# An earlier square root in two split norms, and relu evictions ahead of the squaring in two MLP heads

## What is computed

```python
def rms_norm(x, g):
    y = xf * lax.rsqrt(jnp.mean(xf * xf, axis=-1, keepdims=True) + NORM_EPS)
    return (y * g.astype(jnp.float32)).astype(x.dtype)

def sq_relu_mlp(h, w1, w2):
    return jnp.square(jax.nn.relu(h @ w1)) @ w2

        xl = xl + mod_l[2][:, None, :] * ol
        hl = modulate(rms_norm(xl, norm2_g[i]), mod_l[3], mod_l[4])
        xl = xl + mod_l[5][:, None, :] * sq_relu_mlp(hl, w_ff1[i], w_ff2[i])
```

## Time and profile before

| | |
|---|---|
| median of 3 runs | 2323.17 us (2319.16 to 2323.88) |
| the profiled execution's own time | 2324.08 us |
| its span | 2322.3 us |
| mean granted TensorE clock | 0.972 of full speed |
| TensorE matmul busy | 2212.4 us (95% of the span) |
| VectorE busy | 1370.6 us (59%) |
| ScalarE busy | 794.8 us (34%) |
| GpSimd busy | 719.5 us (31%) |
| chain that ended last | PE 84%, DVE 8%, DMA 3%, ACT 2%, POOL 1%, issue 1% |

### The profile page before, as it was taken

One profiled execution on the slowest core, in us unless ns is written; L12 is line 12 of the kernel. 1 busy time (PEld: TensorE's weight loads), 2 busy tenths in 40 slices (PEclk: granted clock), 3 DMA queues, 4 the chain that ended last, 5 costly groups with the idle time before them and its releaser, 6 DMA issues.

```text
span 2322.3 us, 31326 instructions
## 1 busy us (share of the span) xinstructions
PE 2212.4 (95%) x11982; PEld 1864.6 (80%) x11982; DVE 1370.6 (59%) x1796; ACT 794.8 (34%) x1100; POOL 719.5 (31%) x417
## 2 busy tenths in 40 slices
PE   6999899899999999998999999999997999799997
PEld 5887588899999999784447888887886888688885
DVE  5789842745444444544663745645327551799997
ACT  3211143111111112325663211212323533677775
POOL 1133304233333334322335344444442234111111
PEclk8999979999999999999999999999998999899999
DMA  9699931622222222120002333333231134599996
GB/s 312 198 274 275 284 104 55 262 64 64 63 63 63 63 64 73 57 64 1 10 1 64 101 97 93 99 91 113 74 94 56 60 86 154 204 394 406 399 406 251
DMA packets 254616, 328.53 MB, mean 141 GB/s; under 512 B 15022, under 2 KB 200879, under 8 KB 242231
## 3 DMA queue, kind: packets, MB, share of 16 engines
q1 hardware_dynamic: 242524, 291.65, 38.2%
q0 software_dynamic: 6688, 25.69, 2.9%
q10 hardware_dynamic: 5307, 9.83, 1.1%
HBM read 299.16 MB, written 27.98 MB: 141 GB/s over the span
## 4 chain that ended last, share of the span: by engine, by line
PE 84%; DVE 8%; DMA 3%; ACT 2%; POOL 1%; issue 1%; ACTq 0%; SPq 0%; POOLq 0%; DVEq 0%
PE acc L632 47%; PE acc L3059 8%; PE pb L3077 4%; PE acc L2566 3%; PE pa L2795 2%; PE acc L2781 2%; DMA mod_raw<-in_w_mod 2%; PE pb L2808 2%; PE acc L686 2%; PE acc L668 2%; PE pb L2517 1%; PE acc L2630 1%; DVE hid_hi L1857 1%; PE pa L2456 1%; PE acc L715 1%
## 5 line engine op out<-in xcount | busy, mean ns | idle before, releaser
L571 POOL TENSOR_TENSOR wlo<-raw,whi 128x1024 fp32r<-128x1024 f32 x192 | 480.0, 2502 | 1031.7 <-ACT whi L560 1011.9
L560 ACT ACTIVATE whi<-raw 128x1024 fp32r<-128x1024 f32 x188 | 199.1, 1060 | 892.6 <-PE acc L632 830.5
L632 PE MATMUL acc<-ah,whi 128*128 128x384 f32 (+1 forms) x1256 | 393.3, 361 | 2.6 <-DVE sg L2054 2.6
L632 PE MATMUL acc<-al,whi 128*128 128x384 f32 (+1 forms) x1256 | 388.5, 357 | 0.0
L632 PE MATMUL acc<-ah,wlo 128*128 128x384 f32 (+1 forms) x1256 | 388.4, 357 | 0.0
L632 PEld LDWEIGHTS acc<-ah,whi 128*128 128x128 f32 x1256 | 230.4, 189 | 30.4 <-issue 10.6
L632 PEld LDWEIGHTS acc<-ah,wlo 128*128 128x128 f32 x1256 | 231.3, 188 | 20.1
L632 PEld LDWEIGHTS acc<-al,whi 128*128 128x128 f32 x1256 | 231.1, 188 | 20.1 <-issue 0.5
L1877 DVE SCALAR_TENSOR_TENSOR x<-acc,mod,x 128x512 f32<-128x512 f32 (+1 forms) x174 | 109.7, 658 | 232.2 <-PE acc L632 232.1
L1060 DVE TENSOR_TENSOR expert_lo<-expert_pair,expert_hi 128x1024 fp32r<-128x1024 f32 x192 | 224.4, 1219 | 14.5 <-ACT expert_hi L1055 14.5
L1055 ACT ACTIVATE expert_hi<-expert_pair 128x1024 fp32r<-128x1024 f32 x192 | 201.4, 1059 | 63.5 <-PE acc L3059 40.0
(11 more groups left out here) (495 smaller groups left out, 3672.4 us busy)
## 6 DMA issues: line engine op xcount, KB each, us to landing
raw<-in_w_ff SPq DMA_DIRECT2D x128, 512.0 KB, 3.9
mod_raw<-in_w_mod SPq DMA_DIRECT2D x80, 512.0 KB, 7.9
expert_pair<-in_expert_w_gate SPq DMA_DIRECT2D x32, 1024.0 KB, 7.8
expert_pair<-in_expert_w_up SPq DMA_DIRECT2D x32, 1024.0 KB, 7.5
expert_pair<-in_expert_w_down SPq DMA_DIRECT2D x32, 1024.0 KB, 7.2
raw<-in_w_in SPq DMA_DIRECT2D x30, 512.0 KB, 3.8
raw<-in_conv_w_pw SPq DMA_DIRECT2D x24, 512.0 KB, 12.2
expert_rows_dram<-zero_rows POOLq DMA_DIRECT2D x1, 12288.0 KB, 38.1
```

Of the source, the lines that this page charges most:

```text
L560: e.eng.activation(whi[e.n["q"] % 2][:, :], raw[r][:, :], ACT.Copy).then_inc(S["hi_ready"], 1)
L571: e.eng.tensor_tensor(wlo[b][:, :], raw[e.n["g"] % RING][:, :], whi[b][:, :].bitcast(F32), ALU.subtract).then_inc(S["lo_ready"], 1)
L632: ins = e.eng.matmul(o, w, m, start=keys.index(key) == n, stop=len(keys) - 1 - keys[::-1].index(key) == n)
```

## The change

The change has three parts.

The first: in `split_norm_act` ScalarE takes the early square root behind two late squares (`ahead`) and no longer behind all of the first `FIRST_SPLIT` of them. In norms 1 and 3 three late squares move behind the root. In norms 2 and 4, where `FIRST_SPLIT` is 2, nothing moves.

The second: in both MLP heads VectorE takes the three early results and the late results of slots 0 and 1 out of PSUM first, with the maximum alone (`positive`), into three separate buffers (`rstd`, `tmp` and `tmp3`). Then it squares and splits slots 0 and 1 (`square`), takes slot 2's late result, and squares and splits slot 2. Number and kind of the instructions are the same.

The third: `zero_rows` is set behind the first MLP's head and not in front of it, and GpSimd issues its transfer four low parts (weight slots) later.

```diff
--- before.py
+++ after.py
@@ -823,11 +823,14 @@
                 e.eng.wait_ge(S["sq_added_early"], (KT - 2) * early + i - 2)
             e.eng.activation((squares[(i - 1) % 2] if i else square_sum[0])[:, c0:c1], x[:, i, c0:c1], ACT.Square
                              ).then_inc(S["sq_early"], 1)
-        for i in range(FIRST_SPLIT[n]):
+        ahead = min(2, FIRST_SPLIT[n])
+        for i in range(ahead):
             square_late(i)
         e.eng.wait_ge(S["root_in_early"], early + 1)
         e.eng.activation(token_stat[:, c0 // P:c1 // P], token_stat[:, c0 // P:c1 // P], ACT.Sqrt
                          ).then_inc(S["root_out_early"], 1)
+        for i in range(ahead, FIRST_SPLIT[n]):
+            square_late(i)
         squares_late(-1)
         for i in range(KT):
             e.eng.wait_ge(S["x_scaled_early"], KT * early + i + 1)
@@ -1632,10 +1635,11 @@
 
         slots(e, KT - 1 - SPLIT_SLOTS, low, units=0)
         split_norm_pool(e, 1)
+        split_only(e, 4, low)
         pool.wait_ge(S["prepared"], 4)
         pool.dma_start(yo_d.rearrange("(j p) d -> p j d", p=P),
                        zero_rows[:, :].unsqueeze(1).to_broadcast([P, LIST, D])).then_inc(S["rows_zeroed"], 16)
-        split_only(e, 64 - 2 * SPLIT_SLOTS, low)
+        split_only(e, 60 - 2 * SPLIT_SLOTS, low)
         split_norm_pool(e, 2)
         slots(e, 12 - SPLIT_SLOTS, low, units=0)
 
@@ -1861,13 +1865,33 @@
                 square_of_relu(token_cols(take_unit(e), c0) if c0 else all_cols(take_unit(e)), b, j, c0, TOK).then_inc(S["hid_ready"], 1)
 
             def head():
+
+                def positive(values, j, s0, s1):
+                    free_unit(e, TS(parts[j][:, s0:s1], values, 0.0, None, ALU.max))
+
+                def square(j, s0, s1):
+                    e.step(TT(tmp2[:, s0:s1], parts[j][:, s0:s1], parts[j][:, s0:s1], ALU.mult))
+                    e.step(dve.tensor_copy(hid_hi[0][:, j, s0:s1], tmp2[:, s0:s1]))
+                    return TT(hid_lo[0][:, j, s0:s1], tmp2[:, s0:s1], hid_hi[0][:, j, s0:s1].bitcast(F32), ALU.subtract)
+
+                parts = (rstd, tmp, tmp3)
                 for j in range(SPLIT_SLOTS):
                     values = early_cols(n, take_unit(e)) if j < 2 else after_unit(e, third_cols())
-                    square_of_relu(values, 0, j, EARLY[n][0], EARLY[n][1])
-                for j in range(SPLIT_SLOTS):
-                    square_of_relu(late_cols(n, take_unit(e)), 0, j, LATE[n][0], LATE[n][1]).then_inc(S["hid_ready"], 1)
-                    e.n["g"] += 1
-                    e.n["q"] += 1
+                    positive(values, j, EARLY[n][0], EARLY[n][1])
+                for j in range(2):
+                    positive(late_cols(n, take_unit(e)), j, LATE[n][0], LATE[n][1])
+                dve.wait_ge(S["acc_free"], e.at("u", 2))
+                for j in range(2):
+                    square(j, EARLY[n][0], EARLY[n][1])
+                    square(j, LATE[n][0], LATE[n][1]).then_inc(S["hid_ready"], 1)
+                positive(late_cols(n, take_unit(e)), 2, LATE[n][0], LATE[n][1])
+                dve.wait_ge(S["acc_free"], e.at("u", 2))
+                square(2, EARLY[n][0], EARLY[n][1])
+                square(2, LATE[n][0], LATE[n][1]).then_inc(S["hid_ready"], 1)
+                e.n["g"] += SPLIT_SLOTS
+                e.n["q"] += SPLIT_SLOTS
+                if n == 1:
+                    dve.memset(zero_rows[:, :], 0.0).then_inc(S["prepared"], 1)
 
             def down(chunk, j, b):
                 for n in (2 * j, 2 * j + 1):
@@ -1892,7 +1916,6 @@
         e.step(scales(3, 1, 4, V_N2B))
 
         operand_done(e, 3)
-        dve.memset(zero_rows[:, :], 0.0).then_inc(S["prepared"], 1)
         def last_rows_of_first():
             dve.wait_ge(S["rows_zeroed"], 16)
             split_norm(2, 5, 4, 3, to_stream_part(40), AFFINE[2])
```

## The result

The changed kernel takes 2308.4 us (median of 4 runs, 2302.94 to 2309.11), beside 2321.76 us for the kernel before (4 runs, 2319.16 to 2323.88). The ratio is 0.9938, with a 95% interval of 0.9919 to 0.9957: faster by 0.6%. The median lies 3.4 us over the predicted 2305.0 and inside the range. The profiled execution took 2302.94 us, with a span of 2301.2, and the others up to 2309.11. TensorE is busy for 2202.5 us (96%), where it was 2212.4, carries 87% of the chain that ended last, and its mean granted clock is 0.977. The two profiled executions are 21.1 us apart, the medians 13.4: the profile of after is the fastest of its runs, and that of before is slower than each of the runs beside it.

A forecast was written before the change was run, and what follows sets the result against it. TensorE, busy for 95% of the span, was taken as the bound, so only its waits and the lower clock behind them give time back. 9.6 + 3.7 + 5.6 - 0.8 = 18.1 us from 2323.17 gave 2305, range 2301 to 2309.

The forecast's parts named there:

- First head: First MLP head: TensorE's 7.44 us eviction wait falls to 0.4 and 2.6 of lower clock goes; 9.6 us gained.
- Second head: Second MLP head: the 2.39 us eviction wait and 1.6 of lower clock go, less 0.3 remaining; 3.7 us gained.
- Norm 1's root: Norm 1: root ready before TensorE asks, so the 2.64 us wait and 3.0 of lower clock go; 5.6 us gained.
- Norm 3's root: Norm 3: a new wait before the late squares' sums, with the lower clock behind it; 0.8 us lost.
- The zeros' transfer: GpSimd's 38.1 us transfer moves from the head into the steady part, with weight loads still in time; nothing gained.
- The sum: Whole kernel: 9.6 + 3.7 + 5.6 - 0.8 = 18.1 us gained, from the median 2323.17 to 2305.
- the first: Rival on norm 3: the last addition is not late, 6.1 us instead of -0.8, so 2298; chance 0.12.
- The second: Rival: norm 1 ends as norm 3 does, or 0.4 us waits lower the clock in the heads; 2310; chance 0.15.
- The third: Rival on the heads: the wait only changes its name, TensorE lacking something else at 422; 2311 to 2314; chance 0.05.
- the fourth: Rival on the steady part: slower, the zeros starve the weight ring; chance 0.03.
- the fifth: Rival on the whole kernel: no change that can be measured; chance 0.04.

The follow-up runs named there:

- zeros not moved: The change's roots and evictions against the kernel before, with the zeros set and written at their old place: 2305.43 us, 0.9937.
- Issue alone: The kernel before with only GpSimd's issue of the zeros four low parts later, the memset staying: 2315.66 us, 0.9967.
- earlier additions: The changed kernel with norm 3's last two additions to `x` further ahead: 2302.25 us, 0.9922 against the kernel before.
- roots alone: The kernel before with only the first part of the change, the earlier square roots: 2316.54 us, 0.9978.
- heads alone: The kernel before with only the second part, evictions first in both MLP heads; memset and transfer of zeros left in place: 2308.49 us, 0.995.
- zeros alone: The kernel before with only the third part, memset and transfer of zeros behind the first head: 2316.74 us, 0.9983.

## Why the prediction was right, step by step

**First head, 9.6 us:** 7.34 + 2.30 = 9.64 in every profile that has the evictions first. The mechanism was right; that the sum is exact is luck, since two terms miss by the same 0.3: the remaining wait is 0.10 us and not 0.4, and the lower clock had cost 2.3 and not 2.6. The explanation was incomplete in one step: the cast of 6.08 us was taken as one that GpSimd's low parts hold, but no other instruction of the head stood through two of them, and this one had come while GpSimd was issuing the transfer. The forecast did not rest on that: in "zeros not moved" evictions take 0.41 us during the issue and 0.69 beside a low part, as they do elsewhere.

**Second head, 3.7 us:** 3.75 measured, with a wait of 0.16 us: 2.23 of the wait and 1.5 of the clock. The latter is a draw as well. "Issue alone" has the same wait and pays nothing for it, so that against the mean of the three profiles with a wait of 2.4 us (0, 0.0 and 1.5) the part is worth 3.3.

**Norm 1's root, 5.6 us:** 5.72 in every profile with the root moved. But 3.0 of it was the price of the lower clock in one execution, and other executions of the same code paid less, see below. Set against the mean of the four profiles with the root behind five squares (0, 2.8, 1.5 and 1.5 us ahead of the trace before), it is worth 4.3.

**Norm 3's root, -0.8 us:** the mechanism was right and the sizes were off, so that against the trace before the three profiles of the change gain 0.1 to 0.55 us and lose nothing. The new wait stands where it was forecast, before the sums, with the lower clock behind. TensorE is idle for 3.5 us, 3.12 and the 0.41 for `head_lo`, and not for 4.7. Two terms of the sum differ. TensorE took up the sums at 1261.52, which with the 14.33 us gained until then is 1275.85 in the trace before: 2.15 us before 1278.00, not 1.4. Two `al` tiles slipped in ahead of `head_lo` and not one, though `head_lo`, which was taken as staying in its place, ended 0.6 us later (1256.65 + 14.33 = 1270.98, not 1270.34). And the fall of the clock then cost 1.6 us (2.15 - 0.55) to 2.1 (2.15 - 0.08), not 2.2. Over all profiles of this place the early root gains -0.6 to 1.2 us (mean 0.3 of five) and the late one 0 to 1.3 (mean 0.7 of five), so the root alone is worth some -0.4, which the scatter does not tell from 0.

The rule of the Trainium skill (SBUF — State Buffer, Who interferes with whom), by which the two engines exclude each other for a whole instruction, agrees with the `al` tile at 1254.71, which ends 0.28 us behind GpSimd's low part.

**The zeros' transfer, nothing:** right beside the other two parts, as far as these runs can tell (2305.43 without the move, 2303.5 and 2303.6 with it, intervals overlapping). The transfer took 39.1 us where the earlier trace rows have 38.1, and ScalarE waited for no weights beside it. It was issued at 442.47 us, 23.8 us later than before, where some 30 were forecast. The row of the changed kernel's issues:

```profile
expert_rows_dram<-zero_rows POOLq DMA_DIRECT2D x1, 12288.0 KB, 39.1
```

Alone the move is worth 4.0 us of the first head, since the cast's long stand goes with the issue's place.

**The sum, 18.1 us:** the four terms come to 19.2 to 19.7 us in the profiles. The column "between" takes 1.7 back, in eleven of the twelve other profiles and whatever the edit: the trace before had less of the lower clock between the first head and norm 3 than all of them but one. For the same matmuls it needs 822.0 us there and the change 823.8; "earlier additions", which has the whole change in it, needs 822.0 again. So the 1.7 us are luck of that execution and not a cost of the change. "Start" and "rest", which the change doesn't touch either, add 3.1 to 5.4 us in the three profiles. The medians differ by 13.4, 18.1 and 17.6 us.

That the forecast of 18.1 meets the second of these to the tenth is luck in part. With each price taken from all profiles that have the old wait, and not from the one before, the terms are 4.3 and -0.4 as above, 3.3 for the second head and 9.4 for the first (there "roots alone" has the same wait and pays 0.4 less): an estimate of 16.6 us, inside the spread of the three medians, whose mean is 16.3.

Of the rivals, the first (norm 3 gives 6.1 us) is refuted by the new wait; by the traces 4.3 us are to be had with the additions moved, and 5.3 to 5.5 with the sums moved as well. The second is right in one respect: a short wait can be followed by a lower clock. It did not happen in these heads. The third and the fourth did not occur, and the fifth (no change) is outside the interval.

## What to carry to other kernels

An engine that reads results out of PSUM for TensorE should take all of them that are ready before it works on any, when buffers allow: it costs no instruction and gave 13 of the 18 us. Before a wait is removed, look for what the next instruction behind it will ask for, and move that too: norm 3's root was worth nothing that the scatter lets one see until two additions had moved, and then 4 to 5 us by the traces (1.3 to 3.3 by the medians). Those moves without the earlier root were not run; the wait of 3.3 us for the root would then still stand ahead. A price of the lower clock read from one profile is one draw: take it from several executions of the same place.

## What the runs showed of the hardware

**The same wait costs different amounts.** Behind norm 1's spread, after an identical wait of 2.64 us on the same code, the granted clock over 10 us is 0.69, 1.00 and 0.84 in the kernel before, heads alone and zeros alone. By the table the fall cost 3.1, 0.3 and 1.6 us (5.72 less the row's own gain, less 2.64):

```profile
384.00:394.00 10.00, 9.88 (x33) 8.10 (x34) 8.01 (x17) 4.33 (x10) 4.24 (x3) 0.69 0.19 54
```

```profile
381.60:391.60 10.00, 9.88 (x45) 8.25 (x46) 8.81 (x18) 4.34 (x10) 4.30 (x3) 1.00 0.20 54
```

```profile
380.80:390.80 10.00, 9.88 (x39) 8.31 (x40) 8.29 (x18) 4.35 (x10) 4.25 (x3) 0.84 0.19 54
```

And the lower clock can follow a shorter wait than the prediction's rows had shown. In front of the attention's norm TensorE waits 0.86 us in every kernel. In the change the clock is 0.66 behind it, with earlier additions 1.00:

```profile
953.79 1.02 PE L2721 MATMUL pa<-head_pick,qk_square 128*128 128x2 f32 x8 [0.86 <-ACT qk_square L1378]
```

```profile
955.00:960.00 5.00, 5.00 (x17) 3.69 (x16) 0.00 (x0) 1.88 (x3) 2.27 (x1) 0.66 0.00 0
```

```profile
956.02 1.02 PE L2721 MATMUL pa<-head_pick,qk_square 128*128 128x2 f32 x8 [0.86 <-ACT qk_square L1378]
```

```profile
956.00:962.00 6.00, 5.98 (x30) 4.82 (x31) 0.00 (x0) 2.06 (x4) 2.08 (x1) 1.00 0.01 3
```

The two other profiles of the change show this fall too, and that of heads alone; those of the other kernels don't. What decides it was not tried. The Trainium skill (TensorE: Matmul & The Clock Gate, Part 1) says that at the start of one and the same kernel a different number of matmuls runs at the lower level from run to run; these rows show the like far into a kernel.

**A cast of VectorE that came while GpSimd issued a transfer stood through the two low parts behind the issue.** In the kernel before, and again with the roots moved, it came 0.45 us into an issue of 1.67 us and stood for 6.08 us. No other row of the heads above is held past the low part that was running when it came. The issue before, to be read with the cast at 419.16 and the low parts at 420.40:

```profile
418.71 1.67 POOL L1636 DMA_DIRECT2D expert_rows_dram<-zero_rows  x1 [13.91 <-DVE zero_rows L1895]
```

The issue alone does not do it. In the changed kernel the same issue stands in the steady part, and a difference of VectorE that comes 0.5 us into it takes the same 0.96 us as the others of its size; the next low part starts only at 447.96:

```profile
442.47 1.67 POOL L1640 DMA_DIRECT2D expert_rows_dram<-zero_rows  x1
```

```profile
442.98 0.96 DVE L1862 TENSOR_TENSOR hid_lo<-tmp,hid_hi 128x768 fp32r<-128x768 f32 x1
```

Whether it takes a cast, or a low part right behind the issue, no run separates. The Trainium skill (DMA: Bandwidth & Descriptors, SWDGE vs HWDGE vs iDMA) says that GpSimd writes the descriptors into SBUF; no run here shows the write itself, only the stand and that it goes when the issue is moved.
